# The latent heads' up-projection moved into the third projection chunk, the norms around it reordered, and the first output-weight pieces rounded one a group

## The reference

```
for l in range(DEPTH):                       # DEPTH = 2
    h = rms_norm(x, norm_mix[l]) @ w_in[l]   # 1024 -> 2400, columns split among A, B, C, D
    ...
    # A: c_q = rms_norm(h_a[:192]); c_kv = rms_norm(h_a[192:320]); k_rope = h_a[320:352]
    #    q = c_q @ w_uq ; kv = c_kv @ w_ukv        (the up-projection)
    #    q, k = rms_norm per head, rope on the last 32 of 96 values
    # B: differential attention, C: chunk-relative attention, D: windowed attention with sinks
    heads = jnp.concatenate([rms_norm(o_a, g_out[0]), ...], axis=2)
    x = x + heads.reshape(B, S, D_MIX) @ w_out[l]
    x = x + peer_ffn(rms_norm(x, norm_ffn[l]), peer_wq[l], peer_keys[l], peer_u[l], peer_v[l])
```

## Time and profile before

| | |
|---|---|
| median of 3 runs | 2033.59 us (2032.41 to 2033.64) |
| the profiled execution's own time | 2031.05 us |
| its span, first to last instruction | 2029.3 us |
| mean granted TensorE clock | 0.982 of full |
| PE busy | 1955.0 us, 96% of the span |
| DVE, ACT, POOL busy | 67%, 55%, 28% |
| chain that ended last | PE 88%, DVE 6%, ACT 2%, DMA 2% |

### The profile page before, as it was taken

The page is one execution under the profiler, slowest core; times in us unless marked ns, Lnnn a source line. Parts: engine busy times, 40 slices in busy tenths (PEclk is TensorE's granted clock), DMA queues, the critical chain, the costliest instruction groups (busy, mean ns, idle before and its releaser), DMA issues.

```text
span 2029.3 us, 41824 instructions
## 1 busy us (share of the span) xinstructions
PE 1955.0 (96%) x12772; PEld 1791.4 (88%) x12772; DVE 1363.1 (67%) x3327; ACT 1119.6 (55%) x2444; POOL 576.8 (28%) x452
## 2 busy tenths in 40 slices
PE   7878999999999999999997889999999999999999
PEld 6768999999999888888877789999999998888887
DVE  4764868876767566666667558689677765666665
ACT  5654545456666455555566445455666655555554
POOL 6325310046666000000073253100566660000000
PEclk9888999999999999999999899999999999999999
DMA  7222155544444566676512322555444445555554
GB/s 288 83 98 111 50 189 186 177 155 142 137 140 140 166 239 237 230 255 216 167 46 84 125 84 78 184 184 178 154 135 144 134 145 168 194 195 190 194 194 158
DMA packets 80350, 323.32 MB, mean 159 GB/s; under 512 B 9312, under 2 KB 9824, under 8 KB 77088
## 3 DMA queue, kind: packets, MB, share of 16 engines
q1 hardware_dynamic: 80288, 322.57, 46.5%
HBM read 321.48 MB, written 1.05 MB: 159 GB/s over the span
## 4 chain that ended last, share of the span: by engine, by line
PE 88%; DVE 6%; ACT 2%; DMA 2%; issue 1%; POOL 0%; SPq 0%; DVEq 0%; ACTq 0%
PE ps L551 87%; DMA grid<-in_w_out 1%; PE ps L548 1%; DMA nat<-in_peer_v 1%; ACT wh L896 1%; ACT grid L258 0%; DVE grid L1276 0%; DMA grid<-in_w_in 0%; ACT fh L882 0%; DVE grid L1303 0%; DVE negmax L1307 0%; DVE fl L1180 0%; DVE ss L1343 0%; DVE grid L1270 0%; ACT grid L958 0%
## 5 line engine op out<-in xcount | busy, mean ns | idle before, releaser
L551 PE MATMUL ps<-fh,wh 128*128 128x256 f32 x2304 | 554.6, 289 | 1.8 <-ACT fh L882 1.2
L551 PE MATMUL ps<-fl,wh 128*128 128x256 f32 x2304 | 537.8, 283 | 0.0
L1024 ACT ACTIVATE wh<-nat 128x512 fp32r<-128x512 f32 x520 | 299.1, 623 | 284.7 <-PE ps L551 244.2
L551 PEld LDWEIGHTS ps<-fh,wh 128*128 128x128 f32 x2304 | 426.1, 192 | 4.5 <-ACT fh L882 3.8
L551 PEld LDWEIGHTS ps<-fl,wh 128*128 128x128 f32 x2304 | 425.6, 192 | 0.0
L551 PE MATMUL ps<-wh,gh 128*128 128x512 f32 x1024 | 399.9, 391 | 5.6 <-DVE gl L1572 4.4
L551 PE MATMUL ps<-wl,gh 128*128 128x512 f32 x1024 | 399.6, 390 | 0.0
L551 PE MATMUL ps<-wh,gl 128*128 128x512 f32 x1024 | 399.5, 390 | 0.0
L537 POOL TENSOR_TENSOR wl<-nat,wh 128x512 fp32r<-128x512 f32 x256 | 324.3, 1288 | 183.7 <-PE ps L551 183.7
L1580 DVE TENSOR_TENSOR wl<-nat,wh 128x512 fp32r<-128x512 f32 x504 | 325.9, 688 | 0.4
L551 PE MATMUL ps<-fh,wl 128*128 128x256 f32 x2304 | 324.6, 284 | 1.1 <-DVE wl L1376 1.1
(11 more groups left out here) (174 smaller groups left out, 2193.1 us busy)
## 6 DMA issues: line engine op xcount, KB each, us to landing
nat<-in_peer_u SPq DMA_DIRECT2D x256, 512.0 KB, 3.3
nat<-in_peer_v SPq DMA_DIRECT2D x256, 512.0 KB, 3.3
grid<-in_peer_wq SPq DMA_DIRECT2D x8, 2048.0 KB, 10.3
grid<-in_w_in SPq DMA_DIRECT2D x6, 2048.0 KB, 11.3
grid<-in_w_out SPq DMA_DIRECT2D x2, 4096.0 KB, 13.6
grid<-in_w_in SPq DMA_DIRECT2D x4, 1024.0 KB, 14.0
grid<-in_bias SPq DMA_DIRECT2D x2, 1664.0 KB, 16.6
ab<-in_peer_keys SPq DMA_DIRECT2D x2, 1024.0 KB, 17.2
```

The source lines that it names most:

```text
L551: return nc.tensor.matmul(dst, a, b, start=first, stop=last)
L1024: A(wh[:, s % 2, c], nat[:, s, c], ACT.Copy).then_inc(high_ready, 1)
```

## The change

What it does:

- PE: the up-projection stands after the first four pieces of chunk 2, not after all eight. Its second query product goes to bank 6, not 4, and waits for the eviction of chunk 1. Chunk 3, which writes banks 6 and 7, waits for both copies of the up-projection.
- ACT: the two copies stand after the rounding of piece 23, and the rounding of pieces 24 to 27 follows them.
- DVE: a chunk's norm is in two functions, the sums of squares and the rest. The scaling of the compressed columns stands between the two parts of chunk 1's norm. A's sums, root and first multiplication stand before chunk 2's norm, A's gain and rotation behind it. The two evictions of transposed keys stand together behind the rotation.
- ACT in the groups: the first four `w_out` pieces are rounded one each in steps 7, 8, 9 and 10.
- The counter of DVE's own chain runs on over both layers; this changes no instruction.

```diff
@@ project
+                        if c == 3:
+                            pe.wait_ge(up_copied, past[up_copied] + NT)
@@ up_project
                             if tt == 1:
-                                pe.wait_ge(h_ready, past[h_ready] + 5)
-                            mm(ps[:, 2 + 2 * tt, 0:384], cqt[0:AQK, 0, tk], wuq[:, 0, :], True, False)
-                            mm(ps[:, 2 + 2 * tt, 0:384], cqt[0:AQK, 1, tk], wuq[:, 1, :], False, True).then_inc(up_done, 1)
+                                pe.wait_ge(h_ready, past[h_ready] + 3)
+                            mm(ps[:, 2 + 4 * tt, 0:384], cqt[0:AQK, 0, tk], wuq[:, 0, :], True, False)
+                            mm(ps[:, 2 + 4 * tt, 0:384], cqt[0:AQK, 1, tk], wuq[:, 1, :], False, True).then_inc(up_done, 1)
@@ PE's order
                     turn_compressed()
-                    project(2)
+                    project(2, 0, KD // 2)
                     up_project()
+                    project(2, KD // 2)
                     project(3)
@@ ACT's order
-                    high_pieces(2 * KD + 4, 3 * KD + 4)
+                    high_pieces(2 * KD + 4, 3 * KD)
+                    up_copy(0)
+                    up_copy(1)
+                    high_pieces(3 * KD, 3 * KD + 4)
                     evict(4)
                     evict(5)
-                    high_pieces(3 * KD + 4, 3 * KD + 6)
-                    up_copy(0)
-                    high_pieces(3 * KD + 6, 3 * KD + 7)
-                    up_copy(1)
-                    high_pieces(3 * KD + 7, 4 * KD + 4)
+                    high_pieces(3 * KD + 4, 4 * KD + 4)
@@ ACT in the groups
-                        if i == NG0:
-                            high_pieces(NPI, NPI + 4)
+                        if NG0 + 1 < i < NG0 + 6:
+                            high_pieces(NPI + i - NG0 - 2, NPI + i - NG0 - 1)
@@ DVE's order
-                    norm_chunk(0)
-                    norm_chunk(1)
+                    square_sums(0)
+                    norm_chunk(0)
+                    square_sums(1)
                     dve.wait_ge(cqt_done, past[cqt_done] + 1)
                     v.tensor_scalar(cqt[0:AQK, 0, :], ps[0:AQK, 0, 0:SEQ], gcol[0:AQK, 0:1], None, ALU.mult)
...
+                    norm_chunk(1)
                     dve.wait_ge(lam_ready, past[lam_ready] + 2)
...
-                    norm_chunk(2)
...
                     ch.step(ins)
-                    keys_out(2, 1, 1, 2, 2, 4)
+                    square_sums(2)
+                    norm_chunk(2)
...
                     v.tensor_tensor(x2, r[2], r[3], ALU.add).then_inc(qka_ready, 1)
+                    keys_out(2, 1, 1, 2, 2, 4)
                     keys_out(4, 3, 6, 0, 2, 6)
                     dve.wait_ge(qka_ready, past[qka_ready] + 1)
+                    square_sums(3)
                     norm_chunk(3)
```

More of the change, by code:

```diff
@@ L310, in build @@
                 (260, "high_ready"),
-                (436, "dve_chain"),
                 (1024, "nat_in0 nat_in1 nat_in2 nat_in3")):
@@ L316, in earlier @@
         def earlier(l):
-            return {s: l * PER_LAYER[name] for name, s in names.items()}
+            return {s: l * PER_LAYER[name] for name, s in names.items() if name in PER_LAYER}
         def vcols(kind, n):
@@ L343, in build, with __init__ @@
         class Chain:
-            def __init__(self, eng, s, n):
-                self.eng, self.s, self.n = eng, s, n
+            def __init__(self, eng, s):
+                self.eng, self.s, self.n = eng, s, 0
             def step(self, ins):
@@ L900, in up_copy @@
                         kv = ps[:, tt, :].rearrange("p (h d) -> p h d", h=4)
-                        A(qka[:, tt, 0:4, :], ps[:, 2 + 2 * tt, 0:384].rearrange("p (h d) -> p h d", h=4), ACT.Copy)
+                        A(qka[:, tt, 0:4, :], ps[:, 2 + 4 * tt, 0:384].rearrange("p (h d) -> p h d", h=4), ACT.Copy)
                         A(qka[:, tt, 4:8, 0:NOPE], kv[:, :, 0:NOPE], ACT.Copy)
@@ L1125, in _ @@
             def _(dve):
+                ch = Chain(dve, dve_chain)
                 for l in range(DEPTH):
@@ L1128, in _ @@
                     v = nc.vector
-                    ch = Chain(dve, dve_chain, past[dve_chain])
                     if l == 0:
@@ L1201, in _, with square_sums @@
                     v.tensor_reduce(lamt[:, 0:2], l2[:, :, 0, :], X, ALU.add).then_inc(lam_ready, 1)
-                    def norm_chunk(c):
-                        a = CHUNKS[c][0]
+                    def square_sums(c):
                         groups_ = STATS[c]
@@ L1218, in norm_chunk @@
                             ins.then_inc(sq_used, 1)
+                    def norm_chunk(c):
+                        a = CHUNKS[c][0]
+                        groups_ = STATS[c]
+                        o = sum(k for _, k, _ in groups_)
                         dve.wait_ge(sq_used, past[sq_used] + c * NT + NT)
```

## The result

| | before | after |
|---|---|---|
| median | 2033.17 us (2032.41 to 2033.64, 4 runs) | 2006.77 us (2005.62 to 2008.90, 4 runs) |
| ratio after / before | | 0.9878, 95% interval 0.9866 to 0.9889 |
| the profiled execution | 2031.05 us | 2007.44 us |
| mean granted clock | 0.982 | 0.985 |

What follows compares the result with a forecast made beforehand. PE was taken as the bound, with only its idle and slow stretches in each layer's first half at stake. 2 x 8.0 + 8.4 = 24.4 us gained, median from 2033.59 to 2009.2 us; range 2005 to 2018.

Steps and rivals of the forecast that it cites:

- The two large terms: Before the groups 8.0 us gained a layer; in the groups 8.4 us gained for both layers.
- The up-projection on PE costs nothing and gains nothing there: PE, chunk 2: up-projection runs from 41.3 to 45.3 and the remaining pieces end at 50.8 as before; effect nothing.
- The new wait of chunk 3: Chunk 3 waits for both up-projection copies, done at 46.5, 4 us before it may start; cost nothing.
- the bounds 4.1 and 8.8 of the stage: Range of the gain a layer before the groups; 4.1 if DVE comes late and the clock falls as before.
- the late bound: DVE: chunk 3's norm ready at 74.7 us at the old instruction durations, against 78.95 before the change.
- the relief from POOL: DVE steps freed of simultaneous POOL reads: 0.9 us before A's norm, 0.3 gain, 1.3 rotation, 0.8 its last two.
- PE behind chunk 4: Units 6 to 9 through the first score: 5.2 us from earlier unit 4, 2.5 from clock, 0.3 from chunk 4.
- 2.5 gained, if the clock stays up: PE from unit 4 to the first score takes 3.6 us at full clock instead of 6.1.
- The rival in which the clock falls in spite of the change: Before the groups: clock still falls and DVE comes late; gain 16.6 us, 2017 us; chance 0.14.
- the collisions: Groups: each spread w_out remainder on POOL can hold two-input DVE instructions; 5 us in all, 2014 us; chance 0.12.
- Slower and nothing: Whole kernel: either slower, 2038 us, chance 0.03, or no effect because other waits take each place, 2033 us, chance 0.03.
- The ring: DVE waits for copies, ACT for the up-projection; copies over 16 us late lose, 18 late gives 2038 us; chance 0.03.

Runs made afterwards that it cites:

- Experiment 3: Changed kernel with chunk 2's norm put back whole ahead of A's copies and norm; 2028.31 us, ratio 0.9976 to the kernel before.
- experiment 4: Changed kernel's DVE order, with PE and ACT as before the change and the w_out roundings in step 5; 2033.78 us, ratio 1.0008 to the kernel before.
- experiment 5: Changed kernel with three extra dependent DVE instructions ahead of chunk 3's norm; 2011.16 us, ratio 0.9890 to the kernel before.
- experiment 6: Changed kernel with sixteen extra dependent DVE instructions ahead of chunk 3's norm; 2025.32 us, ratio 0.9968 to the kernel before.
- Experiment 1: Kernel before the change, with only the four w_out roundings moved to one each in steps 7 to 10; 2021.69 us, ratio 0.9947.
- experiment 7: Changed kernel with the three lambda steps moved ahead of chunk 1's root, beside POOL's remainders; 2006.88 us in a single execution.
- the last rows of the table: Changed kernel with w_out roundings in steps 7 to 10 (2006.77 us), four in step 9 (2007.81) or steps 11 to 14 (2007.41).

## Why the prediction was right

**The two large terms held.** Before the groups I had 8.0 a layer and it was 8.8 and 8.9; in the groups 8.4 for both and it was 8.7. The sum, 24.4, stands against 24.8 by the ratio and 26.4 by these stages. That it came within 0.4 is in part luck: the stage terms are 2.0 too small together, and the groups' 8.7 is from two executions. Over all profiles, the six stretches of groups with four roundings in step 5 take 51.7 us on average and the twelve with one each in steps 7 to 10 take 47.7, which is 8.1 for two layers.

**"The up-projection on PE costs nothing and gains nothing there"** held to a tenth: I had its start at 41.3 and the fifth piece at 45.3, and on the old axis they are at 41.35 and 45.35. "The new wait of chunk 3", priced at nothing, held too, the copies being done at 46.9 (46.5 forecast) and no wait showing at chunk 3 or before any of pieces 24 to 31. Experiment 3 adds that, alone, the move doesn't help at all. Two small slips of the working change nothing: 11.2 us for eight pieces is 1.40 each and not 1.38 (a piece takes 1.36 in the trace, the first a little more), and the bounds 4.1 and 8.8 of the stage come out of its own terms as 4.3 and 8.7.

**DVE.** Chunk 3's norm was to be ready at 71.4, with 74.7 as the late bound; it was 72.0. Its terms were less even than the sum. A's norm starts at 47.0, for 46.8. Of the relief from POOL, the lambda steps gave theirs (1.28 to 0.16), the last two rotation steps theirs (0.42 each), the rotation 1.1 of 1.3 (3.47 to 2.38), the gain none of its 0.3: it still takes 2.39. I had said that POOL "has little between 59 and 66.5". It has eight remainders there:

```profile
55.93 9.42 POOL L511 TENSOR_TENSOR wl<-grid,wh 128x512 fp32r<-128x512 f32 x8 [1.17 <-ACT wh L898]
```

They end at 65.35, and only what stands behind them is free. In experiment 4, where POOL is idle at that place, the gain takes 1.82 and the four rotation steps 1.43 in all.

**PE behind chunk 4.** Unit 4 started at 72.7 on the old axis, 6.3 us sooner than before; I had 5.2 for it and 0.3 for chunk 4. This is the term that I had too small: chunk 4 ended 0.8 sooner (units 6 to 9 at 71.0 for 71.8), and the 16 transposes, with no slow clock and no wait behind them, took 1.7 to the next and not 1.95. "2.5 gained, if the clock stays up" was 2.5. I had counted on 0 to 1 us of wait before unit 4; there is none, and the room is the 0.8 of experiment 5. The rival in which the clock falls in spite of the change is not what happened. Experiment 5 shows the clock staying up behind a wait of 0.57, experiment 6 shows it falling behind one of 7.39. Between them the length of the wait alone does not say it: in the kernel before the clock fell behind a wait of 1.85 in the first layer and stayed up behind one of 1.86 in the second, until the wait of 3.37. Experiment 1 has both in one execution, at unit 4 in its two layers, at 1.00 and at 0.50:

```profile
80.03 0.88 PE L548 MATMUL ps<-ident,grid 128*128 128x128 f32 x6 [2.06 <-DVE grid L1235]
1079.96 1.54 PE L548 MATMUL ps<-ident,grid 128*128 128x128 f32 x6 [2.22 <-DVE grid L1235]
```

What decides it stays open.

**The groups.** The wait went as forecast, with 1.4 us to spare (0.9 forecast). Of the collisions DVE's and POOL's timelines show one, where a product that takes 0.22 to 0.27 in the other groups took 0.83 beside the first remainder:

```profile
99.31 0.83 DVE L1341 TENSOR_TENSOR grid<-grid,lists 128x64 f32<-128x64 f32 x1
...
102.33 0.23 DVE L1341 TENSOR_TENSOR grid<-grid,lists 128x64 f32<-128x64 f32 x1
```

```profile
98.78 1.28 POOL L511 TENSOR_TENSOR wl<-grid,wh 128x512 fp32r<-128x512 f32 x1 [18.80 <-ACT wh L898]
```

With the smaller ones it makes some 0.75 us in the first layer, against the 2.5 a layer of that rival and the 0.4 that I had taken. The mechanism of the rival is real; that it is small fits DVE's list, where few instructions have two SBUF inputs (the most frequent long ones, L1312 and L1316, read `ps` and one tile, or one tile alone); no run tests that reason by itself.

**Slower and nothing.** The ring needs copies that come 16 us late; they came 0.4 late. And experiment 6 shows that even 8.25 us of added DVE time ahead of chunk 3's norm leaves the kernel faster than before.

**What stays open.** Stages with the same list of instructions differ: the twelve stretches of groups with the roundings in steps 7 to 10 lie between 46.2 and 48.9 us, and those of one kernel differ as much (46.2 and 48.9 in experiment 7). It goes along with the granted clock near the end of the groups, where DVE is the bound and PE waits often. In all twelve the clock falls to 0.50 there; in the five shortest (46.2 to 47.5 us) it comes back to 1.00 for some 6 or 7 us, in the seven of 48.2 us and more it stays at 0.50 to the end. The changed kernel's first layer is one of the short ones; its low stretch:

```profile
112.00:117.00 5.00, 5.00 (x22) 0.50 0.00 0
```

What decides it was not tried, and which way round cause and effect go is not shown. It means, as do the 2.5 us ahead of the groups in experiment 1, that differences under some 3 us between the last rows of the table mean nothing.

## What to carry to other kernels

When an in-order engine makes two results for one consumer, look at which input comes first and put that work first on all engines at once: here PE's early product and DVE's new order were worth nothing or less apart, and 8.8 us a layer together. When pricing a new wait, subtract the waits behind it that its time pays off; when pricing a removed one, look at the granted clock in the rows behind it and add what it had cost there. Rounding or copying of prefetched data that an in-order engine must do inside a pipeline belongs behind the landing of the transfer, even if that makes it later; how finely it is spread matters much less.

## What the runs showed of the hardware

- A DVE instruction with two SBUF inputs can stand for nearly one whole POOL instruction, even if it is tiny: 1.22 us for one element a partition beside remainders of 1.25, 0.16 alone. With one input: 0.15 in either case.
- Behind a wait of 7.39 or 7.61 us the granted clock is at 0.50 for some us of work (1.54 for 6 transposes that take 0.87 behind the wait of 0.57), and 1.00 a few us later; behind 0.57 us it did not fall. Behind waits of 1.85 to 2.2 us both were seen. I had not expected the fall of experiment 4 to be over before chunk 5.
- A dependent one-input DVE instruction of 128x256 took 0.45 to 0.52 us a step (1.35 for 3, 8.25 for 16), not the 0.3 that I had estimated.
